# Halved last residuals, row sums taken from the loaded input, a two-engine tail and half copies in attention D of a three-layer block

## The chip, the cores and the metric

The kernel runs on one core of a Trainium2 chip. The metric is the device time of one execution in microseconds. All data are float32. TensorE makes the matrix products into PSUM, ScalarE (ACT) and VectorE (DVE) read PSUM and work on it, GpSimd (POOL) splits weights and activations, and SyncE (SP) issues most DMAs.

## The reference

Three layers on a residual stream `h` of 1024 tokens by 1024 features. The first is a four-branch mixer with a feed-forward part, then come one even and one odd attention layer, ahead of which the first block's result is normalized again:

```
h = x
xn = rmsnorm(h, norm_mix_w);  proj = xn @ w_in       # four gated branches
h = h + merged @ w_out
xn = rmsnorm(h, norm_ffn_w);  g, u = split(xn @ w_ffn_in)
h = h + (silu(g) * u) @ w_ffn_out
x = rmsnorm(h, norm_f_w)
x = x + (cat(attention A, attention B) * silu(gate)) @ w_out_e     # even layer
x = x + (cat(attention C, attention D) * silu(gate)) @ w_out_o     # odd layer
```

where `rmsnorm(x, w) = x * rsqrt(mean(x * x) + 1e-6) * w` over the features. Attention D is a differential attention with four heads:

```
p = softmax(q1 @ k1.T * scale) - lam * softmax(q2 @ k2.T * scale);  o = rmsnorm(p @ v)
```

Its queries and keys are projections of the normalized stream, normalized per head and partly rotated.

## The kernel before

The stream lies transposed in SBUF as `H`, eight tiles of 128 features by 1024 tokens. `A(i)` is one of 29 work buffers of that shape. PSUM is used as four banks of 128 x 1024, given out in turn to numbered jobs (`opn`). The last writer of a bank raises `filled`, its last reader raises `freed`, and job n waits for job n - 4 to be freed. Every engine has its program written out in order, and the engines meet only in semaphores.

A product in full precision is made of three: weights and activations are split into a high part (`WH`, `XH`) and a low part (`WL`, `XL`), and 8 x 3 x 2 = 48 matmuls of 512 columns make a tile (`three`, `split_gemm`, `xgemm`, `xhalves`; 24 or 36 where fewer feature tiles go in). SP loads each weight into one of four slots of `WR`; POOL casts it to `WH` (line 3145) and subtracts to `WL` (3147), which lies over `WR`, so a slot is free again when its product is done. `xhalves` gives the same product in two steps of 24 matmuls, one for each half of the tokens. `XL` lies over `H`: before it is written, all of `H` is stored to `spill` in HBM, and it is loaded back later.

At the start the eight tiles of `x` are loaded and transposed by TensorE (470). ScalarE copies each to `H` (1467) and squares four (1474), VectorE squares the other four (2260), and TensorE sums the squares with 64 matmuls (481). A matmul of plain float32 data stands as two passes in the trace; a transpose, and a matmul of split data, as one.

A norm (numbers 0, 1, 3 and 4 in the code) goes as follows. VectorE adds each residual tile (`residual_norm`), ScalarE squares it and stores it (`square`, 1425; in norm 3 there is a second square without weights, 1433, for the final norm of the first block), VectorE sums the squares over the tiles into `A(28)` (and `A(16)`), and TensorE sums over the partitions (`sums`, 431). ScalarE seeds the root (1417, 1419), VectorE refines it in three steps (`newton`), and TensorE spreads it over the partitions (`spread`, 449). VectorE scales (2268), ScalarE casts to `XH` (1440, 1443, 1447), and VectorE and POOL subtract to `XL` by turns. The first pair of products behind a norm, `two_after_norm` (331, 338, 345), takes up each tile as it comes.

The attentions are woven by hand: each step of the attention's loop is followed on every engine by one step of the preparation of the next head (`weave`). In D a head has 16 such steps. TensorE's `prep_d_halves` (404) makes the first half of the keys in step 0 and the second in step 2, and the queries in steps 4 and 6; then come the sums (`hn`). ScalarE's `prep_d_halves` copies and squares the whole tile in steps 3 and 7 by `raw` (1809, 1811), and only then is the bank freed:

```
act.activation(dst[0:m, :], t[0:m, :], ACT.Copy, scale=gain)
act.activation(sq[0:m, :], t[0:m, :], ACT.Square).then_inc(freed[bank(name)], 1)
```

At the end TensorE transposes `H` back, eight transposes for each of eight token tiles (1300), and ScalarE copies each tile out of PSUM (2244) and issues its store (2247).

## Time and profile before

| | |
|---|---|
| median of 3 runs | 3924.49 us (3920.34 to 3936.52) |
| profiled execution | 3924.81 us, span 3923.0 us |
| granted TensorE clock, mean | 0.984 of full |
| TensorE matmul busy | 3751.3 us, 96% |
| VectorE busy | 1818.7 us, 46% |
| ScalarE busy | 1295.7 us, 33% |
| GpSimd busy | 916.9 us, 23% |
| DMA | 215.32 MB, mean 55 GB/s |

The profile is one execution. The span is the time between the first and the last instruction in it. Busy shares are averages over stages with different limits, so what an edit is worth is read at its own place.

### The profile page before, as it was taken

How to read it: one execution, taken by the hardware profiler on the slowest of the kernel's cores; microseconds unless marked ns; L12 is line 12 of the kernel's file. 1: busy time of each engine (PE TensorE's matmuls, PEld its weight loads, DVE VectorE, ACT ScalarE, POOL GpSimd, SP SyncE). 2: the span in 40 equal slices, each digit the busy share in tenths (PEclk: the TensorE clock that was granted, in tenths of full speed). 3: DMA queues.
4: the chain of work that ended last, by engine and by line, in shares of the span. 5: the costliest groups of instructions: out<-in, count | busy, mean ns of one | idle time of the engine just before them, and what ended most of it. 6: DMA issues, size and time to landing. Idle time of an engine off the chain costs nothing.

```text
span 3923.0 us, 51837 instructions
## 1 busy us (share of the span) xinstructions
PE 3751.3 (96%) x21792; PEld 2959.3 (75%) x21792; DVE 1818.7 (46%) x2309; ACT 1295.7 (33%) x1523; POOL 916.9 (23%) x558
## 2 busy tenths in 40 slices
PE   8999999999999999999999999999999999999988
PEld 7778888877788878888888767677676566667767
DVE  6464455624643622101102555655744555456672
ACT  3243333332330111001001234455623666444441
POOL 4212222222233424333333411110023001111101
PEclk9999999999999999999999999999999999999999
DMA  4111111111125421111113221100112001111011
GB/s 144 33 44 54 44 54 44 49 54 46 44 91 185 137 86 43 48 49 48 49 49 103 79 57 48 38 22 7 52 58 62 14 13 26 30 25 25 17 54 68
DMA packets 276813, 215.32 MB, mean 55 GB/s; under 512 B 16273, under 2 KB 255025, under 8 KB 276593
## 3 DMA queue, kind: packets, MB, share of 16 engines
q1 hardware_dynamic: 257808, 150.31, 13.4%
q10 hardware_dynamic: 18784, 61.88, 4.5%
q8 instruction: 163, 2.67, 0.3%
q14 instruction: 58, 0.47, 0.0%
HBM read 170.27 MB, written 37.81 MB: 53 GB/s over the span
## 4 chain that ended last, share of the span: by engine, by line
PE 83%; DVE 9%; ACT 4%; issue 3%; ACTq 0%; DMA 0%; DVEq 0%; SPq 0%
PE ps L356 30%; PE ps L373 17%; PE ps L404 15%; DVE AR L2260 3%; PE ps L1166 2%; DVE SM L3019 2%; PE ps L635 2%; DVE AR L2268 1%; PE ps L338 1%; PE ps L1177 1%; PE ps L1157 1%; PE ps L309 1%; PE ps L449 1%; PE ps L1188 1%; PE ps L1237 1%
## 5 line engine op out<-in xcount | busy, mean ns | idle before, releaser
L3145 POOL CAST WH<-WR 128x1024 fp32r<-128x1024 f32 (+2 forms) x269 | 283.3, 1053 | 2869.2 <-DMA WR<-in_w_in 828.7
L3147 POOL TENSOR_TENSOR WL<-WR,WH 128x1024 fp32r<-128x1024 f32 (+2 forms) x269 | 595.0, 2212 | 21.5
L356 PE MATMUL ps<-XH,WH 128*128 128x512 f32 x1776 | 450.2, 396 | 2.3 <-DVE AR L2260 1.7
L356 PE MATMUL ps<-XH,WL 128*128 128x512 f32 x1776 | 440.5, 390 | 0.0
L356 PE MATMUL ps<-XL,WH 128*128 128x512 f32 x1776 | 438.8, 389 | 0.0
L2260 DVE TENSOR_TENSOR AR<-AR 128x512 f32<-128x512 f32 (+3 forms) x336 | 378.0, 1125 | 54.1 <-ACT AR L1668 38.1
L373 PE MATMUL ps<-ARR,WH 128*128 128x512 f32 x1600 | 395.5, 389 | 5.6 <-ACT ARR L1774 3.4
L356 PEld LDWEIGHTS ps<-XH,WH 128*128 128x128 f32 x1776 | 330.6, 188 | 78.9 <-issue 5.0
L356 PEld LDWEIGHTS ps<-XH,WL 128*128 128x128 f32 x1776 | 332.6, 187 | 72.7
L356 PEld LDWEIGHTS ps<-XL,WH 128*128 128x128 f32 x1776 | 331.1, 186 | 71.8
L373 PEld LDWEIGHTS ps<-ARR,WH 128*128 128x128 f32 x1600 | 300.4, 188 | 69.6 <-ACT ARR L1774 4.6
L2260 DVE TENSOR_TENSOR AR<-AR,ps 128x1024 f32<-128x1024 f32 (+2 forms) x72 | 84.7, 1176 | 550.7 <-PE ps L356 409.3
L3019 DVE TENSOR_REDUCE SM<-ps 128x1 f32<-128x1024 f32 x128 | 156.7, 1224 | 197.9 <-PE ps L1166 116.8
L404 PE MATMUL ps<-XH,WH 128*128 128x512 f32 x864 | 234.6, 415 | 2.9 <-ACT AR L2099 2.3
L2268 DVE SCALAR_TENSOR_TENSOR AR<-ps,AR 128x512 f32<-128x512 f32 (+2 forms) x122 | 59.3, 486 | 343.2 <-ACT AR L1419 228.9
L404 PE MATMUL ps<-XH,WL 128*128 128x512 f32 x864 | 214.1, 390 | 0.0
L404 PE MATMUL ps<-XL,WH 128*128 128x512 f32 x864 | 213.4, 389 | 0.0
L1783 ACT ACTIVATE AR<-ps 128x1024 f32<-128x1024 f32 x22 | 22.6, 1027 | 558.4 <-PE ps L356 558.4
L404 PEld LDWEIGHTS ps<-XH,WH 128*128 128x128 f32 x864 | 159.8, 195 | 56.2 <-issue 19.7
L404 PEld LDWEIGHTS ps<-XH,WL 128*128 128x128 f32 x864 | 162.7, 188 | 34.8
L373 PE MATMUL ps<-ARR,WL 128*128 128x512 f32 x736 | 187.7, 389 | 0.0
L404 PEld LDWEIGHTS ps<-XL,WH 128*128 128x128 f32 x864 | 162.2, 188 | 33.7
(261 smaller groups left out, 5165.6 us busy)
## 6 DMA issues: line engine op xcount, KB each, us to landing
WR<-in_w_in SPq DMA_DIRECT2D x78, 512.0 KB, 3.8
WR<-in_w_ffn_in SPq DMA_DIRECT2D x44, 512.0 KB, 3.8
gates<-AR ACTq DMA_DIRECT2D x32, 512.0 KB, 2.9
AR<-gates SPq DMA_DIRECT2D x32, 512.0 KB, 3.6
H<-spill ACTq DMA_DIRECT2D x32, 512.0 KB, 5.5
WR<-in_w_in_e SPq DMA_DIRECT2D x26, 512.0 KB, 3.9
spill<-H ACTq DMA_DIRECT2D x24, 512.0 KB, 2.6
WR<-in_w_in_o SPq DMA_DIRECT2D x23, 512.0 KB, 3.8
```

What stands on the lines that cost most here:

```text
L309: mm = pe.matmul(pt[0:m, h * 512:h * 512 + 512], WR[0:kp, w % 4, k, 0:m], rhs(k)[0:kp, h * 512:h * 512 + 512], start=k == 0, stop=k == nk - 1)
L338: pe.matmul(pt[:, h * 512:h * 512 + 512], wp[:, slot, k, :], XH[:, k, h * 512:h * 512 + 512], start=False, stop=False, skip_group_check=True)
L356: mm = pe.matmul(pt[0:m, h * 512:h * 512 + 512], wp[:, slot, k, 0:m], xp[:, k, h * 512:h * 512 + 512], start=i == 0, stop=i == 3 * KD - 1)
L373: mm = pe.matmul(pt[:, h * 512:h * 512 + 512], wp[:, w % 4, k, :], xp(k)[:, h * 512:h * 512 + 512], start=i == 0, stop=i == 3 * nk - 1)
L404: mm = pe.matmul(pt[:, h * 512:h * 512 + 512], wp[:, w % 4, k, :], xp[:, k, h * 512:h * 512 + 512], start=i == 0, stop=i == 3 * KD - 1)
L635: mm = pe.matmul(out, x1[r, c], later, start=True, stop=True)
L1166: mm = pe.matmul(pt[:, h * 512:h * 512 + 512], q(p, m)[0:96, rows], k(p, m)[0:96, h * 512:h * 512 + 512], start=True, stop=True)
L2260: return v.tensor_tensor(o, x, y, op)
L2268: return v.scalar_tensor_tensor(out=o, in0=x, scalar=s, in1=y, op0=op0, op1=op1)
L3019: v.tensor_reduce(SM[:, 34 + m:35 + m], PS[bank(("S", b, m))][:, :], AX.X, ALU.max)\
L3145: pool.tensor_copy(hi, full).then_inc(s_whi, 1)
L3147: pool.tensor_tensor(lo, full, hi, ALU.subtract).then_inc(s_wsplit, 1)
```

## The change

At the start ScalarE squares the loaded tiles as they lie, token by partition, with a row sum into one column each, and a single transpose of these columns takes the place of the 64 matmuls. VectorE makes all eight copies to `H`. The mask is loaded behind two weights, and `two_after_norm` waits for each weight's split by itself. In the norms 1, 3 and 4 the last residual tile is added in two halves, the first when the first half of its product is done; TensorE sums the first seven tiles' squares and the last one's as separate groups. In norm 3 the sums for the final norm move behind the first pair of products. At the end seven eighths of the first three tiles are transposed ahead of the last residual, ScalarE and VectorE copy by turns, and SP issues the stores. In attention D, ScalarE takes the halves of keys and queries each behind its own half product.

```diff
-                pe.wait_ge(s_wsplit, nsplit[0])
                 splits.append(("norm", norm))
                 for h in range(2):
                     pe.wait_ge(s_xhi if h else s_xhi_half, t * KD + 1 if h else t + 1)
-                    for pt, n, slot in places:
+                    for j, (pt, n, slot) in enumerate(places):
+                        if not h:
+                            pe.wait_ge(s_wsplit, nsplit[0] - 1 + j)
...
+                    if halves and h == 0:
+                        mm.then_inc(s_half_done, 1)
...
+                    if not h and first_done is not None:
+                        mm.then_inc(first_done, 1)
...
-                pe.wait_ge(s_sumsq, norm_turn(i) * (KD - 1))
+                t = norm_turn(i)
+                pt, n = opn(("norm", i))
+                pe.wait_ge(freed[n % 4], n // 4)
+
+                def add(kind, x, first, last):
+                    c = CW[kind]
+                    for j in range(4):
+                        for g in range(2):
+                            mm = pe.matmul(pt[g * 64:g * 64 + 64, 0:P], CST[:, c + 6 - 2 * j:c + 70 - 2 * j],
+                                           x[:, (4 * g + j) * P:(4 * g + j + 1) * P], start=first and j == 0, stop=last and j == 3)
+                    return mm
+
+                pe.wait_ge(s_sumsq, t * (KD - 2))
+                add("w1024", A(28), True, False)
                 if i == 3:
-                    pe.wait_ge(s_sumsq_plain, KD - 1)
-                    sums(("norm", 3), ("w1024", "weps"), [A(28), A(16)])
-                    sums(("norm_f",), "w1024", [A(16)])
-                else:
-                    sums(("norm", i), "w1024", [A(28)])
+                    pe.wait_ge(s_sumsq_plain, KD - 2)
+                    add("weps", A(16), False, False)
+                pe.wait_ge(s_nsq, t * (KD + 1))
+                mm = add("w1024", A(27), False, i != 3)
+                if i == 3:
+                    pe.wait_ge(s_nsq_plain, KD + 1)
+                    mm = add("weps", A(18), False, True)
+                mm.then_inc(filled[n % 4], 1)
...
-            for t in range(NT):
-                g, i, c = t // 4, t % 4, CW["w1024"]
-                if t in DVE_SQUARES:
-                    pe.wait_ge(s_xsq, DVE_SQUARES.index(t) + 1)
-                else:
-                    pe.wait_ge(freed[bank(("x", t))], turn(("x", t)))
-                for f in range(KD):
-                    mm = pe.matmul(pt[g * 64:g * 64 + 64, 0:P], CST[:, c + 6 - 2 * i:c + 70 - 2 * i],
-                                   A(16 + t)[:, f * P:f * P + P], start=i == 0 and f == 0, stop=i == 3 and f == KD - 1,
-                                   skip_group_check=True)
-            mm.then_inc(filled[n % 4], 1)
+            pe.wait_ge(s_xsq, NT)
+            pe.transpose(pt[:, 0:P], A(26)[:, 0:P], IDENT).then_inc(filled[n % 4], 1)
...
+                sums(("norm_f",), "w1024", [A(16), A(18)])
+                xgemm(("va", 0), cols(wie, EVA))
                 spread(("norm_fb",), A(19))
-                xgemm(("va", 0), cols(wie, EVA))
...
-            for k in range(4):
-                n = J["wout_o"] + 4 + k
+            for k in range(3, 7):
+                n = J["wout_o"] + k
                 pe.wait_ge(freed[n % 4], n // 4 + 1)
-            for t in range(NT):
+
+            def turn_out(t, fs):
+                pt, n = PS[bank(("out", t))], J[("out", t)]
+                for f in fs:
+                    mm = pe.transpose(pt[:, f * P:f * P + P], H[:, f, t * P:t * P + P], IDENT)
+                return mm, n
+
+            for t in range(3):
+                opn(("out", t))
+                turn_out(t, range(KD - 1))
+            pe.wait_ge(s_half_added, 4)
+            for t in range(3):
+                mm, n = turn_out(t, [KD - 1])
+                mm.then_inc(filled[n % 4], 1)
+            n = J["wout_o"] + 7
+            pe.wait_ge(freed[n % 4], n // 4 + 1)
+            for t in range(3, NT):
                 pt, n = opn(("out", t))
                 pe.wait_ge(freed[n % 4], n // 4)
-                for f in range(KD):
-                    mm = pe.transpose(pt[:, f * P:f * P + P], H[:, f, t * P:t * P + P], IDENT)
+                mm, n = turn_out(t, range(KD))
...
+                if w == 2 and not mask_in:
+                    sp.dma_start(MSK[:, :, :].rearrange("p a b -> p (a b)"), a["msk"]).then_inc(s_msk_in, 16)
+                    mask_in.append(True)
...
+            for t in range(NT):
+                sp.wait_ge(freed[bank(("out", t))], turn(("out", t)))
+                sp.dma_start(a["out"][0, t * P:t * P + P, :], A(16 + t)).then_inc(s_out_in, 16)
+            sp.wait_ge(s_out_in, 16 * NT)
...
-            def square(i, k):
-                if k >= 3:
-                    act.wait_ge(s_sumsq, (norm_turn(i) - 1) * (KD - 1) + k - 2)
-                act.activation(A(26 + k % 2) if k else A(28), H[:, k, :], ACT.Square,
+            def square(i, k, c=slice(0, L), last=True):
+                t = norm_turn(i) - 1
+                if k >= 3 and c.start == 0:
+                    act.wait_ge(s_sumsq, t * (KD - 2) + k - 2)
+                act.activation((A(26 + k % 2) if k else A(28))[:, c], H[:, k, c], ACT.Square,
                                scale=par("nf", k) if i == 3 else 1.0).then_inc(s_nsq, 1)
                 act.wait_ge(s_nsq, tick(s_nsq))
                 if i == 3:
                     if k == 0:
                         act.wait_ge(s_part, KD)
-                    if k >= 3:
+                    if k >= 3 and c.start == 0:
                         act.wait_ge(s_sumsq_plain, k - 2)
-                    act.activation(A(17 + k % 2) if k else A(16), H[:, k, :], ACT.Square).then_inc(s_nsq_plain, 1)
+                    act.activation((A(17 + k % 2) if k else A(16))[:, c], H[:, k, c], ACT.Square).then_inc(s_nsq_plain, 1)
                     act.wait_ge(s_nsq_plain, tick(s_nsq_plain))
-                act.dma_start(a["spill"][k], H[:, k, :]).then_inc(s_spilled, 16)
+                if last:
+                    act.dma_start(a["spill"][k], H[:, k, :]).then_inc(s_spilled, 16)
...
+                    if k == KD - 1:
+                        act.wait_ge(s_half_added, norm_turn(i))
+                        square(i, k, slice(0, 512), False)
                     act.wait_ge(freed[n % 4], n // 4 + 1)
-                    square(i, k)
+                    square(i, k, slice(512 if k == KD - 1 else 0, L))
...
+            logs()
+            act.wait_ge(s_xsq_zero, 1)
             for t in range(NT):
-                act.wait_ge(filled[bank(("x", t))], turn(("x", t)))
-                pt = PS[bank(("x", t))]
-                copy = act.activation(H[:, :, t * P:t * P + P], pt[:, :].rearrange("p (f i) -> p f i", i=P), ACT.Copy)
-                if t in DVE_SQUARES:
-                    copy.then_inc(freed[bank(("x", t))], 1)
-                    act.wait_ge(freed[bank(("x", t))], turn(("x", t)))
-                else:
-                    copy.then_inc(s_act_step, 1)
-                    act.wait_ge(s_act_step, tick(s_act_step))
-                    act.activation(A(16 + t), pt[:, :], ACT.Square).then_inc(freed[bank(("x", t))], 1)
-                    act.wait_ge(freed[bank(("x", t))], turn(("x", t)))
-            logs()
-            act.wait_ge(s_par_in, 32)
+                act.wait_ge(x_in[t], 16)
+                c = 64 * (t // 4) + 2 * (t % 4)
+                act.activation(A(16 + t), A(t), ACT.Square, scale=1.0 / 32, accum_out=A(26)[:, c:c + 1]).then_inc(s_xsq, 1)
+                act.wait_ge(s_xsq, tick(s_xsq))
...
+            def first_half(name, nth, dst, sq=None, gain=1.0):
+                act.wait_ge(s_d_half, nth)
+                t = PS[bank(name)]
+                act.activation(dst[:, 0:512], t[:, 0:512], ACT.Copy, scale=gain).then_inc(s_act_step, 1)
+                act.wait_ge(s_act_step, tick(s_act_step))
+                if sq is not None:
+                    act.activation(sq[:, 0:512], t[:, 0:512], ACT.Square).then_inc(s_act_step, 1)
+                    act.wait_ge(s_act_step, tick(s_act_step))
+
+            def second_half(name, dst, sq=None, gain=1.0):
+                act.wait_ge(filled[bank(name)], turn(name))
+                t = PS[bank(name)]
+                last = act.activation(dst[:, 512:L], t[:, 512:L], ACT.Copy, scale=gain)
+                if sq is not None:
+                    last.then_inc(s_act_step, 1)
+                    act.wait_ge(s_act_step, tick(s_act_step))
+                    last = act.activation(sq[:, 512:L], t[:, 512:L], ACT.Square)
+                last.then_inc(freed[bank(name)], 1)
+                act.wait_ge(freed[bank(name)], turn(name))
+
             def prep_d_halves(h):
-                yield from pause(3)
+                k, q = A(10 + h % 2), A(8 + h % 2)
+                yield
                 act.wait_ge(s_rope_tmp, 14 + 2 * h)
-                raw(("kd", h), A(10 + h % 2), A(22), gain=par("gkd"))
-                yield
-                rotated(A(28), A(10 + h % 2), (0, 64), 8, s_rot_in[1])
-                yield from pause(3)
-                raw(("qd", h), A(8 + h % 2), A(7), gain=par("gqd"))
+                first_half(("kd", h), 2 * h - 1, k, A(22), par("gkd"))
+                yield from pause(2)
+                second_half(("kd", h), k, A(22), par("gkd"))
+                yield
+                rotated(A(28), k, (0, 64), 8, s_rot_in[1])
+                yield
+                first_half(("qd", h), 2 * h, q, A(7), par("gqd"))
+                yield from pause(2)
+                second_half(("qd", h), q, A(7), par("gqd"))
                 root()
                 yield
-                rotated(A(27), A(8 + h % 2), (0, 64), 8, s_rot_in[0])
+                rotated(A(27), q, (0, 64), 8, s_rot_in[0])
...
+            def last_residual(n, nth, between):
+                v.wait_ge(s_half_done, nth)
+                TT(H[:, KD - 1, 0:512], H[:, KD - 1, 0:512], PS[n % 4][:, 0:512], ALU.add).then_inc(s_half_added, 1)
+                v.wait_ge(s_half_added, nth)
+                between()
+                v.wait_ge(filled[n % 4], n // 4 + 1)
+                TT(H[:, KD - 1, 512:L], H[:, KD - 1, 512:L], PS[n % 4][:, 512:L], ALU.add).then_inc(freed[n % 4], 1)
+                v.wait_ge(freed[n % 4], n // 4 + 1)
...
+                    if k == KD - 1:
+                        last_residual(n, norm_turn(i), lambda: add_square(i, KD - 2))
+                        continue
...
+            v.memset(A(26)[:, 0:P], 0.0).then_inc(s_xsq_zero, 1)
+            v.wait_ge(s_xsq_zero, 1)
+            for t in range(NT):
+                v.wait_ge(filled[bank(("x", t))], turn(("x", t)))
+                v.tensor_copy(H[:, :, t * P:t * P + P], PS[bank(("x", t))][:, :].rearrange("p (f i) -> p f i", i=P))\
+                    .then_inc(freed[bank(("x", t))], 1)
...
+            for t in range(1, NT, 2):
+                v.wait_ge(filled[bank(("out", t))], turn(("out", t)))
+                v.tensor_copy(A(16 + t), PS[bank(("out", t))][:, :]).then_inc(freed[bank(("out", t))], 1)
+                v.wait_ge(freed[bank(("out", t))], turn(("out", t)))
```

Of the pieces with `if k == KD - 1`, the first is in ScalarE's `norm_after`, the second in VectorE's `residual_norm`. The last product ahead of each norm is called with `halves` set. ScalarE's `prep_a0` now takes queries and keys first, then the seeds of the final norm, and then the bias load (`in_rpb`), which came first before.

How the rows of TensorE's program stand around norm 3 (`L373`/`L378` is the last product ahead of it, `L431`/`L440`/`L470` are summing matmuls and `L449`/`L458` spreads), before:

```order
L373 MATMUL ps<-ARR_54,WH 128x512 x2
L431 MATMUL ps<-AR,CST 64x128 x24
L449 MATMUL ps<-AR,CST 128x128 x8
...
L345 MATMUL ps<-XL,WH 128x512 x32
L449 MATMUL ps<-AR,CST 128x128 x8
L356 MATMUL ps<-XH,WH 128x512 x8
```

and in the changed kernel:

```order
L378 MATMUL ps<-ARR_54,WH 128x512 x2
L470 MATMUL ps<-AR,CST 64x128 x32
L458 MATMUL ps<-AR,CST 128x128 x8
...
L350 MATMUL ps<-XL,WH 128x512 x32
L440 MATMUL ps<-AR,CST 64x128 x16
L361 MATMUL ps<-XH,WH 128x512 x8
```

There are 32 summing matmuls ahead of the spread where 24 stood, and 16 behind the pair of products where the second spread stood.

ScalarE's program at the start of attention D (`L2139`/`L2200` are the exponentials, `L2128`/`L2189` copies of turned probabilities, and the rows with `PAR` copies of keys), before:

```order
L2139 ACTIVATE AR,SM<-ps,SM,AR 128x1024 x4
L1809 ACTIVATE AR<-ps,PAR 128x1024
L1811 ACTIVATE AR<-ps 128x1024
L2128 ACTIVATE AR<-ps 128x1024
L1803 DMA AR<-AR 8x1024
```

and in the changed kernel:

```order
L2200 ACTIVATE AR,SM<-ps,SM,AR 128x1024 x2
L2112 ACTIVATE AR<-ps,PAR 128x512
L2115 ACTIVATE AR<-ps 128x512
L2200 ACTIVATE AR,SM<-ps,SM,AR 128x1024 x2
L2121 ACTIVATE AR<-ps,PAR 128x512
L2125 ACTIVATE AR<-ps 128x512
L2189 ACTIVATE AR<-ps 128x1024
L1835 DMA AR<-AR 8x1024
```

The first half of the keys stands between the first two pairs of exponentials, the second half where the whole pair stood.

## Rows read from the trace of the kernel before

**Rows 1.** The page, busy time by engine: us, share, instructions

```profile
PE 3751.3 (96%) x21792; PEld 2959.3 (75%) x21792; DVE 1818.7 (46%) x2309; ACT 1295.7 (33%) x1523; POOL 916.9 (23%) x558
```

**Rows 2.** Chain that ended last, 0 to 70 us: start, us, what

```profile
18.07 13.82 PE ps L481 x128
...
36.70 3.75 PE ps L331 x8
...
61.58 8.61 PE ps L356 x38
```

**Rows 3.** Timeline of the start: start, us, instructions, [idle before <-releaser]

```profile
14.99 2.12 PE L470 MATMUL ps<-CST,AR 128*128 128x128 f32 x16 [0.46 <-ACT AR L1474]
...
19.05 1.04 POOL L3145 CAST WH<-WR 128x1024 fp32r<-128x1024 f32 x1 [18.60 <-DMA WR<-in_w_in]
...
20.17 3.21 POOL L3147 TENSOR_TENSOR WL<-WR,WH 128x1024 fp32r<-128x1024 f32 x1
...
50.28 3.24 POOL L3147 TENSOR_TENSOR WL<-WR,WH 128x1024 fp32r<-128x1024 f32 x1
```

**Rows 4.** Windows at the start: length, busy by engine, then clock, DMA share, GB/s

```profile
31.00:32.00 1.00, 0.88 (x9) 0.63 (x6) 0.00 (x0) 0.03 (x1) 0.00 (x0) 1.00 1.04 414
...
33.00:34.00 1.00, 0.21 (x2) 0.21 (x4) 0.67 (x3) 0.00 (x0) 0.00 (x0) 1.00 0.57 221
```

**Rows 5.** Groups of instructions by shape: busy, mean ns | idle before

```profile
L2703 DVE COPY AR<-ps 128x1024 f32<-128x1024 f32 x8 | 9.8, 1224 | 76.0 <-PE ps L373 76.0
...
L1440 ACT ACTIVATE XH<-AR 128x512 fp32r<-128x512 f32 x4 | 2.5, 630 | 14.8 <-DVE AR L2268 14.8
```

**Rows 6.** Chain of norm 1: start, us, what

```profile
1455.48 1.23 DVE H L2260
...
1459.27 1.97 PE ps L431 x16
...
1463.08 2.10 PE ps L449 x16
```

**Rows 7.** One window of norm 1, columns as in rows 4

```profile
1459.00:1460.00 1.00, 0.73 (x8) 0.73 (x10) 0.21 (x1) 0.46 (x1) 0.00 (x0) 0.67 0.90 369
```

**Rows 8.** Chain of norm 3 and behind it: start, us, what

```profile
2198.87 3.70 PE ps L431 x32
...
2204.40 1.19 PE ps L449 x16
...
2242.93 1.02 PE ps L431 x16
```

**Rows 9.** TensorE's waits, whole span: us in total, times, longest

```profile
PE ps L431 <- DVE AR L2260: 7.9, 2, 3.9
...
PE ps L431 <- issue: 6.5, 1, 6.5
```

**Rows 10.** TensorE's waits in attention D, columns as in rows 9

```profile
PE ps L431 <- ACT AR L1811: 7.8, 3, 2.7
...
PE ps L1237 <- ACT AR L1811: 1.5, 1, 1.5
...
PE ps L1223 <- ACT AR L1811: 1.3, 2, 0.6
```

**Rows 11.** Timeline of attention D, first head: ScalarE and VectorE

```profile
3491.26 1.02 ACT L2128 ACTIVATE AR<-ps 128x1024 f32<-128x1024 f32 x1 [3.13 <-PE ps L1223]
...
3500.78 1.11 ACT L1809 ACTIVATE AR<-ps,PAR 128x1024 f32<-128x1024 f32 x1
...
3502.34 1.28 DVE L2268 SCALAR_TENSOR_TENSOR AR<-AR,SM 128x1024 f32<-128x1024 f32 x1
```

**Rows 12.** Timeline of the tail

```profile
3907.66 6.30 PE L1300 MATMUL ps<-CST,H 128*128 128x128 f32 x56 [1.61 <-DVE H L2260]
...
3908.82 1.02 ACT L2244 ACTIVATE AR<-ps 128x1024 f32<-128x1024 f32 x1 [53.60 <-PE ps L1300]
3909.87 0.34 ACTq L2247 DMA_DIRECT2D out<-AR  x1
```

**Rows 13.** DMA queue, 3900 to 3923 us: packets, MB, share of 16 engines

```profile
q10 hardware_dynamic: 1152, 4.19, 45.6%
```

49 lines of the change are left out of this document (25 added, 24 removed).

## The prediction

> **What bounds the kernel now.** I read the busy shares first. TensorE is busy for 96% of the span [rows 1] and no other engine for half of it, so a change pays only where TensorE stands waiting, and there it pays in full, because what follows is packed TensorE work. I then listed TensorE's waits. The places that the diff touches are on that list, and I read the chain of each.
>
> At the start TensorE spends 13.82 us on 128 passes of square sums, the first product starts at 36.70, and the first pair of products ends at 61.58 [rows 2]. At norm 1 the last product ends at 1455.35, 0.13 ahead of the residual add; three VectorE passes follow, the sums run from 1459.27 to 1461.24, and the spread takes 2.10 [rows 6]. The same wait of 3.9 stands twice in the list, for norm 1 and norm 4 [rows 9]. At norm 3 the wait is 6.5, and 32 passes of sums take 3.70 [rows 8, 9]. In D TensorE waits 7.8 us in three places and 2.8 in three more for ScalarE's square of keys or queries, line 1811 [rows 10]. In the tail eight copies and stores stand one behind the other on ScalarE.
>
> **The start.** Removed: 64 summing matmuls (13.82) and ScalarE's copies. Added: eight squares with a row sum on ScalarE straight from the loaded tiles, eight PSUM copies on VectorE, one transpose. A VectorE copy of this shape takes 1.22 [rows 5]. The last two tiles are turned from 14.99 on, in 2.12 us, with hardly a gap [rows 3], so the last tile lands at about 16.0. The last copy then ends at 18.4, and the last square at 17.3. What the row sum costs is not shown for this form: from nothing to the square's own time again for one tile, 18.3. From there the old steps remain: root, spread, first scale and cast took 36.70 − 31.89 = 4.8. TensorE could start at about 22.5.
>
> It then needs split weights. The first came in at 19.05 and took 1.04 + 3.21 to split [rows 3]. With the 512 KB mask behind two weights, both land 1.3 us earlier at 414 GB/s [rows 4]. Weight 1 is split at about 21.3 to 22.1, weight 2 at 25 to 26.5. The new wait is per weight, so two products (0.9 us) fit between, and TensorE ends the pair 24.9 (61.58 − 36.70) after 24 to 25.6, at 49 to 50.5.
>
> What is late next is the low parts. They are written over H, so they wait for the store of H, and the DMA engines are full until 33.6 [rows 4]. The change moves the same bytes, so that end stays. VectorE and GpSimd then start four low parts each, side by side, where GpSimd's subtract takes 3.24 [rows 3]. So GpSimd is done at 33.6 + 4 × 3.3 = 46.8, just in time for TensorE. Only then does it split weight 3, 1.04 + 2.4, until 50.5. The third product starts at 50.6 against 61.58: **11.0 saved**. Bounds: 9 if every GpSimd step has its slow price, 13 if the store ends earlier.
>
> **Norms 1 and 4.** The last residual is added in two halves, the first half and its square beside the second half of the product. That half lasts at least 2.7 us (norm 4: 12 matmuls of 8.61/38 = 0.227 [rows 2]); the first half's add (0.7) and the waiting sum pass (1.24) fit in it. Behind the product remain 0.13, a half add of about 0.68 (half of 1.23 and a fixed part), a half square (the cast of that shape takes 0.63 [rows 5]) and about 0.08 of hand-over, 1.5 in all, then 16 passes. Where TensorE had just worked these took 1.02 [rows 8]; the other 16 run before. They end 2.5 behind the product, against 1461.24 − 1455.35 = 5.9: 3.4 saved. The spread took 2.10 at norm 1 and 1.19 at norm 3 [rows 6, 8], half and full clock. TensorE's first idle stretch shrinks from 3.9 to 0.5, so I take full clock: 0.9. **4.3 each, 8.6 for both.** The clock fell to half within the 1459 to 1460 row, four us after the last product [rows 7].
>
> **Norm 3.** Four groups of 16 passes now stand on the path, 4.1 us at full clock, three of them able to run while VectorE and ScalarE finish their halves (0.13 + 0.68 + 2 × 0.63 + 0.08 = 2.2). The sums end 4.1 behind the product, against 6.5 + 3.7 = 10.2: 6.1 saved. The sums of the final norm come later, two groups behind the first pair of products: 2.0 of TensorE added. **Net 4.1.** The bias load and its two VectorE adds move behind keys and queries, four full copies of about 1.03 on ScalarE, so 4 us later. The gate's product, 48 matmuls or 10.9 us, covers them, so I cost them at nothing; without that cover they would cost up to 4.
>
> **Attention D.** For each of three heads ScalarE now copies and squares the first halves while TensorE makes the second half product, and only two half-size instructions stay behind it. A full pair took 1.11 + 1.03 [rows 11]. A half from PSUM is not shown. Its bounds are half of that and all of it; I take 0.63 each, the cast's row [rows 5]: 1.3 against 2.2, 0.9 saved behind every product. For keys the waits of 1.5, 0.65 and 0.65 shrink by 0.9, 0.65, 0.65. For queries 2.6 shrinks by 0.9 in two heads; in the first the probabilities come only at 3503.62 [rows 11], 0.5 behind today's start of the sums, so 0.5. That is 4.5, and I take **4.0** for new small delays. The new first halves stand where ScalarE idles: 3.13 us ahead of the next copy at the place of the first head's queries [rows 11]. Bounds: 0, if ScalarE's next copy is delayed as often as a wait is cut, and 5.
>
> **The tail.** Three tiles are transposed for seven eighths ahead of the last residual. But 21 transposes of 6.30/56 = 0.11 take 2.4 us, so the first copy starts 2.6 behind the last product, against 2.76 now (3908.82 − 3906.06) [rows 12]. What shrinks is the stretch after it: copies on two engines and stores from SyncE come every 0.7 us and not every 1.44, and then the DMA engines bind. Today 13.1 us pass from the first store to the end; the transfers fill 45.6% of 23 us, 10.5 us, of it [rows 13]. Packed, with 0.8 for the first and last edge, they take 11.3. **Saved 1.9**, bounds 0 and 3.
>
> The Trainium skill speaks against that term: "DMA: Bandwidth & Descriptors", section "Where 436 GB/s comes from", says that transfers between HBM and SBUF are held to some 358 GB/s. By it the 4.19 MB take 11.7 us, the tail gives 0.7, and the result would be 3896. The row of 414 GB/s in a store to HBM contradicts it [rows 4], so the row decides.
>
> **Sum.** 11.0 + 8.6 + 4.1 + 4.0 + 1.9 = 29.6. The profiled execution took 3924.8 us (span 3923.0 and 1.8 around it), 0.3 above the median of the runs. 3924.8 − 29.6 = 3895.2, so **3895 us**.
>
> **Rivals.**
> - *The clock.* It was down when the sums began at norms 1 and 3 [rows 7, 8]. If it still is, the sums cost 1.0 more and the spreads 0.9 more in norms 1 and 4, and norm 3 up to 3.9 more: 3895 + 7.7 = 3903. If it never falls, the first eight products take 1.8 in place of 3.75 [rows 2] and the next five 1.1 less: 3 us twice and some 1.5 at norm 3, so 3887. For the first speaks that only small matmuls with gaps fill the stretch; against it, that the idle is shorter. The Trainium skill, "TensorE: Matmul & The Clock Gate", Part 1, calls the throttled clock the default that activity releases; that leaves both open.
> - *The start gives less.* If the store of H ends later (its issue now stands behind a VectorE copy) or the low parts slow each other further, the third product comes at 55 and D gives nothing: 3895 + 4.4 + 4.0 = 3903.
> - *Attention D turns slower and eats everything.* ScalarE works in order. At six places it now waits for a half product, with the next copy of turned probabilities and the exponentials queued behind it, for which TensorE waits. If each wait held the attention back by a whole half product, 24 × 0.23 = 5.5 us, that is 33, against 25.6 saved elsewhere: 3895 + 4 + 33 = 3932, slower than before. It decides from 4.3 us per place. Against it: the half product is issued a half step earlier, and the idle stretch of 3.13.
> - *The wait moves in norm 3.* The bias adds come too late: 4 us, 3899, inside the forecast's own range.
>
> **How the numbers follow.** Forecast 0.62 (3889 to 3901), clock down or a poorer start 0.20 (3901 to 3908), clock never down or the store earlier 0.12 (3882 to 3889), D slower 0.03, the rest 0.03. The range 3885 to 3906 leaves out some 2 in 10. Half a per cent, 20 us, is about what a measurement of this kernel tells from no change; the gain falls under it only in the last two cases and in a pile of misses. Faster 0.93, same 0.04, slower 0.03.
>
> **What the profile after would show.** The third product near 50.6, behind GpSimd's split and not behind the input. In norms 1 and 4 the sums end 2.5 behind the last product and the spread takes 1.2; the granted clock tells which case it is. In norm 3 no row at half clock in the sums. In D no wait for the square of keys in the second and third head, and 1.7 in place of 2.6 for queries. In the tail a solid stretch of DMA at over 400 GB/s. The prediction is wrong if TensorE waits at a new place: for first halves in D, for the bias in norm 3, or for the third weight beyond 52.

## The result and the profile after

The changed kernel takes 3909.41 us (median of 5 runs, 3899.55 to 3914.30), beside 3923.89 for the kernel before in the same rounds: a ratio of 0.9949 with a 95% interval of 0.9932 to 0.9966. It is faster by 14.5 us at the medians, half of the 29.6 that the prediction summed up, and the time lies 3.4 us above the upper end of its range, 3906. The profiled execution took 3912.17 us with a span of 3910.3, so the two spans that are compared here differ by 12.7.

It was timed again in two later batches, 6 runs each: 0.9956 (0.9942 to 0.9971) and 0.9937 (0.9920 to 0.9954). A least-squares fit over all runs of all kernels, with one level for each batch, gives the change a gain of **20.8 us, plus or minus 3.0** (17 runs of it, 61 of the kernel before). One run scatters by 5.2 us (standard deviation) whatever the kernel. So the forecast of 29.6 is some 9 us too high. That the first five runs were poor ones isn't shown: 14.5 and 20.8 differ by no more than five runs on either side allow.

First the page of the changed kernel, busy time by engine, to lay beside [rows 1]:

```profile
PE 3745.8 (96%) x21745; PEld 2950.7 (75%) x21745; DVE 1848.5 (47%) x2318; ACT 1291.3 (33%) x1538; POOL 908.8 (23%) x558
```

TensorE is busy for 5.5 us less, and the rest of the 12.7 is waiting that went away. VectorE works 30 us more.

**The start**, the chain that ended last (start, us, what), beside [rows 2]:

```profile
11.78 1.23 DVE H L2414
...
18.07 1.24 DVE H L2414
...
25.11 10.36 DMA spill<-H
...
35.59 2.39 POOL XL L3235
...
44.74 3.26 POOL XL L3235
...
48.06 1.92 POOL WH L3225
...
50.05 2.38 POOL WL L3227
...
52.56 17.51 PE ps L361 x76
```

The 13.82 us of square sums are gone; VectorE's eight copies end at 19.3. The chain then leaves TensorE: the last store of H lands at 35.46, four low parts follow, then the split of weight 3, and only then the third product, at 52.56 instead of 61.58. The prediction had this chain, with a landing at 33.6 and a cast of 1.04.

TensorE itself is close behind. Its timeline around the start of the first pair of products and around its end, with GpSimd and VectorE between 18 and 23 us:

```profile
22.48 2.08 PE L458 MATMUL ps<-AR,CST 64*128 64x128 f32 x16 [5.18 <-DVE AR L2327]
26.42 0.76 PE L336 MATMUL ps<-XH,WH 128*128 128x512 f32 x1 [1.86 <-ACT XH L1481]
...
43.78 7.42 PE L350 MATMUL ps<-XL,WH 128*128 128x512 f32 x32
...
52.56 2.08 PE L361 MATMUL ps<-XH,WH 128*128 128x512 f32 x8 [1.37 <-POOL WL L3227]
```

```profile
18.84 2.34 POOL L3227 TENSOR_TENSOR WL<-WR,WH 128x1024 fp32r<-128x1024 f32 x1
...
19.65 2.77 DVE L2327 SCALAR_TENSOR_TENSOR AR<-AR 128x128 f32<-128x128 f32 x2
```

The pair begins at 26.42, not between 24 and 25.6, and ends at 51.20. So GpSimd's chain holds the third product back by 1.4 us and no more.

**Norm 1**, the chain from the last product on, beside [rows 6]:

```profile
1456.61 0.70 DVE H L2319
...
1457.39 0.64 ACT AR L1465
...
1458.40 1.28 ACT L1445
...
1459.70 0.38 ACT AR L1456
...
1461.52 1.30 PE ps L458 x16
...
1464.65 3.75 PE ps L336 x8
```

One full add, one full square and one full sum have become halves. In their place ScalarE's table load (L1445, 1.28) now stands on the chain; before, it began at 1458.17, beside VectorE's pass, and the sums ended 1.8 us behind it.

**Norm 3**, TensorE's timeline, beside [rows 8]:

```profile
2189.33 3.71 PE L470 MATMUL ps<-AR,CST 128*64 128x128 f32 x64
2194.91 1.16 PE L458 MATMUL ps<-AR,CST 64*128 64x128 f32 x16 [1.87 <-DVE AR L2327]
```

The sums begin right behind the last product and not 6.5 us later, and 64 passes take 3.71, as long as 32 took before at half clock [rows 8].

**The merge ahead of norm 1** is a place that the change doesn't touch. TensorE's waits there, 1340 to 1378 us, in the kernel before and in the changed one (us, times, longest):

```profile
PE ps L373 <- ACT ARR L1765: 2.2, 1, 2.2
```

```profile
PE ps L378 <- ACT ARR L1803: 4.9, 2, 4.8
```

**Where the 12.7 are.** I took the same TensorE instruction in both traces and subtracted the start times. The change is ahead by 8.9 us at 62, 8.6 at 285, 3.8 at 1350, and it is *behind* by 1.0 at 1373. From there it gains 3.5 around norm 1, 3.5 around norm 3, 3.0 in the stretch with norm 4, 3.2 in attention D. So in this pair of traces each of these places gains, and 9.5 us vanish between 285 and 1373, in code that is the same in both.

**Theories.** A: the gain of the start is real, but is given back between 285 and 1373, because everything there runs in another phase (other waits, another order of VectorE and GpSimd, other falls of the clock). B: nothing is given back; single executions differ by this much in that stretch, and the profile of before was a good one. C: the local gains are an illusion of alignment, and the start is all there is.

### The profile page after: what moved, and what is told of

The parts are those of the page before. It is cut to its first block, busy times and chain, and to the rows that moved or that the text cites. A ratio compares the mean times of both kernels' runs of the same rounds, so it can differ in the third digit from the quotient of the medians.

```text
span 3910.3 us, 51791 instructions
## 1 busy us (share of the span) xinstructions
PE 3745.8 (96%) x21745; PEld 2950.7 (75%) x21745; DVE 1848.5 (47%) x2318; ACT 1291.3 (33%) x1538; POOL 908.8 (23%) x558
## 4 chain that ended last, share of the span: by engine, by line
PE 83%; DVE 9%; ACT 4%; issue 3%; POOL 0%; DMA 0%; ACTq 0%; SPq 0%; DVEq 0%; POOLq 0%
PE ps L361 30%; PE ps L378 17%; PE ps L411 15%; DVE AR L2319 2%; PE ps L1183 2%; DVE SM L3092 2%; PE ps L651 2%; DVE AR L2327 1%; PE ps L1194 1%; PE ps L1174 1%; PE ps L1205 1%; PE ps L313 1%; PE ps L458 1%; PE ps L1254 1%; PE ps L343 1%
## 5 line engine op out<-in xcount | busy, mean ns | idle before, releaser
L378 PE MATMUL ps<-ARR,WH 128*128 128x512 f32 x1600 | 396.0, 390 | 8.3 <-ACT ARR L1803 4.9
L378 PEld LDWEIGHTS ps<-ARR,WH 128*128 128x128 f32 x1600 | 300.4, 188 | 72.6 <-ACT ARR L1803 5.7
L378 PE MATMUL ps<-ARR,WL 128*128 128x512 f32 x736 | 189.3, 392 | 0.0
```

Source lines behind the costliest of these rows:

```text
L378: mm = pe.matmul(pt[:, h * 512:h * 512 + 512], wp[:, w % 4, k, :], xp(k)[:, h * 512:h * 512 + 512], start=i == 0, stop=i == 3 * nk - 1)
```

## The experiments

**The change in three parts.** Each kernel is that of before with the diff's blocks of one part: `start_only` (norm 0, copies, mask, waits by weight), `norms_only` (norms 1, 3, 4), `d_tail` (attention D and the tail). Their core:

```
start_only   + act.activation(A(16 + t), A(t), ACT.Square, scale=1.0 / 32, accum_out=...)
             - for t in DVE_SQUARES: ...
norms_only   + last_residual(n, norm_turn(i), lambda: add_square(i, KD - 2))
d_tail       + first_half(("kd", h), ...); second_half(...)
             + for t in range(1, NT, 2): v.tensor_copy(A(16 + t), ...)
```

> Only the start of the change: norm 0 from squares of x itself, first-tile waits one by one, mask load behind the second weight. Nothing else differs from the kernel before. Theory A (the start's gain is real, but is given back in unchanged code between 285 and 1373 us, by other waits on VectorE and clock falls at other places): the third product starts 8 to 10 us earlier, at 1373 us no more than 2 us of it is left, and the time is within 3 us of the kernel before. Theory B (the gain stays, and what the whole change lacked is chance of the clock in single executions): at 1373 us and at the end 7 to 10 us are left, time 3914 to 3917 when the kernel before has 3924. Theory C (the norms and D gave nothing and the start is all that was gained): 12 to 15 us faster.

> Only norms 1, 3 and 4 are changed (halved last residual and square, one addition fewer, sums in two parts, final norm's sums behind the first product); the start, attention D and the tail are as before. Theory A: nothing is saved up to 1455 us, then about 3 us at norm 1, 6.4 at norm 3 and 4 at norm 4, together 13 to 14 us, all of it still there at the end (3910 when the kernel before has 3924). Theory B: the same 13 to 14 us. Theory C: under 3 us. If a gain ahead of a stage is given back there in general (theory A carried further), less than 9 us stay at the end though the three places show their 13.

> Only attention D (first halves of keys and queries copied and squared behind their own half product) and the tail (halved last residual, output tiles copied by ScalarE and VectorE in turn, stores by SyncE) are changed. Theories A and B: nothing up to 3372 us, then 3.5 us in attention D and 1.2 to 1.9 us in the tail, 4.5 to 5.5 us in all (3919 when the kernel before has 3924). Theory C: under 1 us. Rival to both: D's gain in the whole change came from another phase of the weave, and alone the change of D gives 0 or a loss of 1 to 3 us.

> The changed kernel once more, in the same rounds as its three parts, for its time beside theirs and for a second profiled execution. If the parts add up, its gain is the sum of the gains of the three partial kernels to within 3 us. Theory A: 14 to 18 us faster than before, and the loss between 285 and 1373 us stands in this execution too, by 6 to 10 us. Theory B: a profiled execution with less time at half clock keeps 7 us or more of the start at 1373 us.

Measured against 29 runs of the kernel before (3926.25):

```
kernel        median    ratio (95%)
start_only    3921.46   0.9986 (0.9973 to 0.9998)
norms_only    3919.75   0.9987 (0.9975 to 0.9998)
d_tail        3923.30   0.9992 (0.9981 to 1.0004)
after_again   3909.53   0.9956 (0.9942 to 0.9971)
```

The fit over all batches gives 5.6, 7.2 and 3.6 us, each plus or minus 3.6: together 16.4 against 20.8, the same within the scatter. The norms alone gain more than theory C allows (under 3 us in its own condition), and the start alone gains far less than its 12 to 15, so C falls. The gain of `d_tail` is not clear of zero in its time. Two expectations missed: `norms_only` was to give 13 to 14 us and gave 7.2, and `start_only` fell between the ranges of theories A and B. `start_only` is ahead by 9.1 us at 62 and 3.2 at 1373, which looks like theory A. But `d_tail`, which equals the kernel before up to 3372 us, is 8.7 us behind it at 1350, and `norms_only` 3.4. That is what theory B says. In the one trace of `norms_only` 11.1 us stand in the three stretches with a norm, and 8.4 of them are left at the end, because of the stretch ahead of 1373.

**Who comes first, VectorE or GpSimd.** In the merge, VectorE adds the last branch to the accumulator while GpSimd splits the first weights of the output product. VectorE's and GpSimd's timelines of the changed kernel, 1350 to 1360 us (start, us, instruction):

```profile
1351.91 2.00 DVE L2319 TENSOR_TENSOR ACC<-ACC,AR 128x1024 f32<-128x1024 f32 x1
1353.94 3.31 DVE L2319 TENSOR_TENSOR XH<-ACC,ARR 128x1024 fp32r<-128x1024 f32 x1
...
1358.54 3.17 DVE L2319 TENSOR_TENSOR ACC<-ACC,AR 128x1024 f32<-128x1024 f32 x1
```

```profile
1351.79 1.04 POOL L3225 CAST WH<-WR 128x1024 fp32r<-128x1024 f32 x1 [6.43 <-DMA WR<-in_w_out]
1352.91 3.26 POOL L3227 TENSOR_TENSOR WL<-WR,WH 128x1024 fp32r<-128x1024 f32 x1
```

The same two engines in the first profile of the kernel before:

```profile
1355.73 1.22 DVE L2260 TENSOR_TENSOR ACC<-ACC,AR 128x1024 f32<-128x1024 f32 x1
1356.99 1.95 DVE L2260 TENSOR_TENSOR XH<-ACC,ARR 128x1024 fp32r<-128x1024 f32 x1
...
1361.17 1.23 DVE L2260 TENSOR_TENSOR ACC<-ACC,AR 128x1024 f32<-128x1024 f32 x1
```

```profile
1355.81 2.04 POOL L3145 CAST WH<-WR 128x1024 fp32r<-128x1024 f32 x1 [6.63 <-DMA WR<-in_w_out]
```

Read the starts. Where GpSimd's cast begins 0.12 us ahead of VectorE's add, it takes 1.04 and the add 2.00; the next two adds of SBUF tiles are the second ones too, and need up to 3.31 for 1.22 us of work. Where it begins 0.08 us behind, the cast takes 2.04 and the add its 1.22. The blocked instruction ends 1.08 us after the other in both of the first pairs (1351.79 + 1.04, then 1353.91; 1352.91 + 3.26, then 1357.25), so it waits for the whole of it. The Trainium skill, "SBUF — State Buffer", section "Who interferes with whom", states that a VectorE instruction with two SBUF inputs contends with a GpSimd instruction that reads SBUF, and that issue order decides who blocks. By that rule, the trace agrees: an add that reads PSUM and one SBUF tile keeps its 1.22 at 1357.29, beside GpSimd's cast of 1.92 at 1356.24.

Three edits follow. `merge_order` makes GpSimd wait with that split for VectorE's sixth add, and moves the table load of norm 1 up:

```
+ if w == first_wout[0]:
+     pool.wait_ge(s_acc, 2 * KD + 6)
...
+ logs()
  norm_after("wout", 1)
```

`late_split` puts a wait into the kernel before, which lets GpSimd begin with the seventh product, so that its subtraction comes just ahead of VectorE's add:

```
+ if w == first_wout[0]:
+     n = J[("br", 3, 6)]
+     pool.wait_ge(filled[n % 4], n // 4 + 1)
```

`spill_both` tests the start. It is the changed kernel, with the odd stores of H issued by ScalarE instead of SyncE:

```
- for k in range(KD):
+ for k in range(0, KD, 2):
      sp.dma_start(a["spill"][k], H[:, k, :]).then_inc(s_spilled, 16)
...
+ for k in range(1, KD, 2):
+     act.dma_start(a["spill"][k], H[:, k, :]).then_inc(s_spilled, 16)
```

`all_three` is the changed kernel with this edit and both edits of `merge_order`.

> The changed kernel, but the eight stores of the residual at the start are issued by two engines: SyncE the even tiles, ScalarE the odd ones, between its seed for norm 0 and its wait for the first normalised half, where it stood idle for 7.4 us. Theory A (the start gave 8.9 and not 11.0 us because SyncE took 6.45 us to issue the eight stores, so that the last landed at 35.46 and not at 33.6 us, and GpSimd's low parts, the split of weight 3 and the third product wait for it in a chain): the stores land 1.5 to 3 us earlier, GpSimd's first low part starts so much earlier, the third product starts at 50 to 51 us instead of 52.56. Rival (the transfer itself is bound by its rate, 4 MB whoever issues it): the last store lands within 0.5 us of 35.46 and the third product stays at 52 to 53 us. The time as a whole: up to 2 us faster than the changed kernel, which five rounds can hardly tell.

> The changed kernel with two edits at two places: GpSimd splits the first weight of the output product only when VectorE has added the sixth tile of the last branch (one wait), and ScalarE loads its table for logarithm and exponential ahead of the squares of norm 1 instead of between the last square and the seed. Theory A (in the changed kernel GpSimd's first split began 0.12 us ahead of VectorE's addition, and from there on VectorE's additions had to wait for GpSimd's: 2.0 to 3.2 us instead of 1.22; before it began 0.08 us behind it, and GpSimd's were the ones that waited): the additions on that chain fall back to 1.2 to 2.0 us, TensorE's wait for the last merged tile falls from 4.8 to 2.2 us, 3 to 4 us are kept at 1372 us. Rival (the additions are slow for what they touch, or TensorE's product ends late for another reason): the wait stays at 4 to 5 us. For the table: if it is exposed, 1.28 us disappear between the last square and the logarithm and norm 1 ends 0.6 to 1.3 us earlier; if the sums on TensorE end no earlier than the table, nothing. The time: 3 to 5 us faster than the changed kernel, 3904 to 3907 when that has 3909.

> The changed kernel with all three: stores on two engines, the ordered split and the earlier table. Theory A: the three gains add, 2 + 3.5 + 1 us, 3901 to 3905 when the changed kernel has 3909 and the kernel before 3926, a ratio of 0.993 to 0.995. Rival (a gain ahead of 1373 us is not kept, since the order of VectorE and GpSimd and the clock fall differently in each program): within 3 us of the changed kernel.

> The kernel before with one wait more: GpSimd begins the split of the first weight of the output product only when the seventh product of the last branch is done, 4 us later than it does by itself, so that its subtraction begins just ahead of VectorE's addition of that tile instead of behind it. No product waits for this split (it is needed some 10 us later). Theory A (who begins first decides): VectorE's additions beside the splits grow from 1.22 to 2 us and more, TensorE's wait for the last merged tile grows from 2.2 to 4 or 5 us, 2 to 3 us are lost at 1372 us. Rival (the order does not matter, or the split is only needed later): the wait stays at 2.2 us. Up to 1350 us the kernel is that of before, so its profile is also a second look at the stretch from 285 to 1350 us: if the profile of before was a lucky one there, this one is 4 us or more behind it at 1000 us.

Measured against 15 runs of the kernel before (3928.17):

```
kernel        median    ratio (95%)                 lost 1350-1373   TensorE's wait
spill_both    3906.04   0.9940 (0.9927 to 0.9954)   4.8              4.8
merge_order   3903.11   0.9938 (0.9924 to 0.9951)   1.5              2.4
all_three     3904.70   0.9947 (0.9933 to 0.9960)   0.9              2.4
late_split    3925.94   1.0000 (0.9991 to 1.0009)   3.5              4.2
```

The order decides the wait, shown from both sides: put right, the wait is 2.4 in `merge_order` and `all_three`, put wrong, it is 4.2. VectorE's rows of `late_split`:

```profile
1360.26 3.33 DVE L2262 TENSOR_TENSOR ACC<-ACC,AR 128x1024 f32<-128x1024 f32 x1
1363.62 1.95 DVE L2262 TENSOR_TENSOR XH<-ACC,ARR 128x1024 fp32r<-128x1024 f32 x1
```

and of `merge_order`:

```profile
1358.24 1.51 DVE L2322 TENSOR_TENSOR ACC<-ACC,AR 128x1024 f32<-128x1024 f32 x1
1359.79 1.95 DVE L2322 TENSOR_TENSOR XH<-ACC,ARR 128x1024 fp32r<-128x1024 f32 x1
```

In `late_split` the add grew from 1.22 to 3.33 and TensorE's wait to 4.2, as theory A's price for the order had it, though nothing waits for the split itself. That place cost it 3.5 us in the trace, but its time of 1.0000 doesn't show them. Its interval reaches to 3.5 us, just so, and the kernel before, against which it is timed, falls into the same order in some of its own executions (below).

The start, GpSimd's rows of `spill_both`:

```profile
34.82 12.41 POOL L3240 TENSOR_TENSOR XL<-AR,XH 128x1024 fp32r<-128x1024 f32 x4 [10.32 <-DMA spill<-H]
47.30 1.91 POOL L3230 CAST WH<-WR 128x1024 fp32r<-128x1024 f32 x1
49.29 2.37 POOL L3232 TENSOR_TENSOR WL<-WR,WH 128x1024 fp32r<-128x1024 f32 x1
```

The low parts begin 0.8 us earlier (34.82 instead of 35.59) and the third product at 51.81. But `merge_order`, where SyncE alone issues the stores and needs 7.22 us for it, begins them at 34.88. So two issuing engines bring nothing, and theory A of that expectation (1.5 to 3 us earlier) fell. The rival's numbers were a little off too: the last store lands at 34.70, 0.76 ahead of 35.46, and the third product comes at 51.81 and not at 52 to 53. But its cause holds, that the issue does not set the landing, and the kernel before shows it best. There the last store is issued at 29.0, 3.9 us later than in the changed kernel, and this is its row and the time to its landing:

```profile
L1344 SPq DMA_DIRECT2D spill<-H x1: 1204/1204/1204, 29.0 to 29.0; - x1
...
DMA to landing us min/median/max: 6.3/6.3/6.3
```

It lands at 35.3, where those of the changed kernel land. The low parts begin between 34.8 and 35.6 in every kernel with the new start.

The table: behind the last square the logarithm begins 1.68 us after in the changed kernel and 1.18 after in the second execution of the ordered one (below), so 0.5 us of the 1.28 were exposed. `all_three` is no faster than either of its parts: 22.8 us ahead of the kernel before in the fit, beside 23.0 for `spill_both`, each plus or minus 5.2.

**Chance or program.** So far the changed kernel, `spill_both` counted with it, had come out badly at the merge in three executions of three, and the kernel before, with its three parts, well in four of four. So both ran again, unchanged (`before_again`, `after_third`), the ordered kernel as `order_again`, and `start_norms`, which is the changed kernel without the blocks of attention D and the tail:

```
- first_half(("kd", h), ...); second_half(...)
+ raw(("kd", h), A(10 + h % 2), A(22), gain=par("gkd"))
- for t in range(1, NT, 2): v.tensor_copy(A(16 + t), ...)
```

> The kernel before, unchanged, for one more profiled execution of it. If the profile of before was ahead of its usual course between 285 and 1350 us (which the kernels that equal it there were behind by 1.2 to 10 us), this one is behind it by 2 to 8 us at 1350 us, and GpSimd's first split of the output weights begins just behind VectorE's addition (wait of TensorE 2.2 us). If it is within 1 us of the first profile all along, the stretch costs the other kernels something that their code brings.

> The changed kernel without its edits in attention D and in the tail, that is the start and the norms together. If the start and the norms are what puts GpSimd's split ahead of VectorE's addition, TensorE's wait for the last merged tile is 4.8 us as in the changed kernel, and the time is 4 us above it (3 of attention D and 1.3 of the tail). If it takes the whole program, the wait is 2.2 us, 3.5 us of the race come back and the time is within 1 us of the changed kernel: 3909 to 3910 when that has 3909.

> The changed kernel once more, as the base for the ordered one on the same chip. 16 to 19 us faster than the kernel before; GpSimd's split ahead of VectorE's addition and TensorE's wait of 4.8 us once more, if this belongs to the program and not to chance in one execution.

> The changed kernel with the ordered split and the earlier table, once more and beside the changed kernel on the same chip. 3.5 us from the order and 0.6 us from the table: 4 us faster than the changed kernel (2 to 6 with the spread of five rounds), 20 to 23 us faster than the kernel before. If the clock takes the gain back elsewhere, it is within 1 us of the changed kernel.

Measured against 11 runs of the kernel before (3929.89); the first is a single execution:

```
kernel        median    ratio (95%)                 lost 1350-1373   TensorE's wait
before_again  3931.39   -                           4.8              4.8
start_norms   3910.14   0.9954 (0.9939 to 0.9968)   4.7              4.8
after_third   3902.68   0.9937 (0.9920 to 0.9954)   1.2              2.2
order_again   3906.78   0.9939 (0.9926 to 0.9952)   0.2              2.4
```

The same program of the kernel before now has, at the same place:

```profile
1353.96 1.04 POOL L3145 CAST WH<-WR 128x1024 fp32r<-128x1024 f32 x1 [6.41 <-DMA WR<-in_w_out]
1354.10 1.98 DVE L2260 TENSOR_TENSOR ACC<-ACC,AR 128x1024 f32<-128x1024 f32 x1
```

and the changed kernel, in its third execution:

```profile
1351.59 1.23 DVE L2319 TENSOR_TENSOR ACC<-ACC,AR 128x1024 f32<-128x1024 f32 x1
1351.70 2.02 POOL L3225 CAST WH<-WR 128x1024 fp32r<-128x1024 f32 x1 [6.66 <-DMA WR<-in_w_out]
```

So one and the same program does both. It is a toss in each execution, and it goes with the time that the weight takes from its issue to its landing: 4.7 to 4.8 us in the five executions that came out badly, 4.9 to 5.3 in the five that came out well, among the ten without a wait of mine there. Theory A's mechanism is right, and its claim that the change brings the bad order about each time is wrong. Whether the change shifts the odds stays open: four of six executions with the new start came out badly and one of four without it, too few to tell. My expectation for `before_again` named only the better case, and missed; so did the one for `after_third`, which had the wait of 4.8 and 16 to 19 us. Against the first profile of before, the second one is 3.1 us behind at 1373 and 6.6 at the end.

The ordered kernel (`merge_order`, `order_again`) is 23.1 us faster than the kernel before in the fit, plus or minus 3.8, the changed one 20.8 plus or minus 3.0. It never lost the toss in three executions, `all_three` among them, but 2 us can't be told from none here. The expectation for `order_again`, 4 us faster than the changed kernel, missed: on that chip the changed kernel's median was 4.1 us lower. That the order is worth its 3.5 us in the time is not shown.

**All traces together.** With fourteen traces each stretch can be taken as a mean over the kernels that have an edit, less the mean over those that don't. All are differences to the first trace of before, in us, with twice the standard error:

```
stretch (us of before)      with edit    without     edit's gain      forecast
0-62       the start         9.30 (9)     0.47 (5)    8.8 +- 0.5       11.0
62-285                      -0.59        -0.14       -0.4 +- 0.5        0
285-1350                    -2.78        -2.22       -0.6 +- 4.2        0
1373-1473  norm 1            3.72 (9)     0.76 (5)    3.0 +- 0.7        4.3
2190-2245  norm 3            3.51         0.58        2.9 +- 0.3        4.1
2900-3372  norm 4            4.56        -0.34        4.9 +- 1.6        4.3
3372-3852  attention D       3.41 (8)    -0.69 (6)    4.1 +- 1.5        4.0
3852-end   the tail         -0.31        -0.97        0.7 +- 1.1        1.9
```

The third row bears on theory A: kernels with the new start lose 2.8 us between 285 and 1350 beside the first profile of before, kernels without it 2.2. A give-back is not shown there, and up to some 5 us of it can't be excluded. Single executions of code that is the same reach from 8.7 behind to 1.6 ahead in that stretch, which is enough to make the 4.8 us that the first pair of traces lost there. The local gains sum to 23.4 (with -1.0 for the second and third rows, and without stretches that no edit touches), which the timing's 20.8 plus or minus 3.0 holds.

## Where the prediction was right and where it was wrong, by its steps

The direction and the places were right. The sum of 29.6 was too large by some 9 us, above all in the terms of the start and of the norms 1 and 3.

- **The start, 11.0 forecast, 8.8 measured.** The chain was right: the third product comes behind GpSimd's split, not behind the input. "The change moves the same bytes, so that end stays" was right too: the last store lands at 35.3 before and at 34.7 to 35.5 with the change. What failed is the time that was read for it. 33.6 is where the DMA share falls off [rows 4], and the landing, which is what GpSimd waits for, comes 1.7 us behind that. The step of 46.8 to 50.5 also had a cast of 1.04 where 1.92 was measured: it begins beside VectorE's last low part (45.77 to 49.07), as the uncontended row I took [rows 3] did not. The low parts gave 0.8 back, 12.41 for four instead of 13.2. A second step failed beside it, and would have held the third product at 51.2 even with a landing at 33.6: the pair of products was to begin at 24 to 25.6 and began at 26.42. "Root, spread, first scale and cast took 4.8" was read where GpSimd stood still. Now VectorE's last two steps of the root run beside GpSimd's split and take 2.77 instead of 0.62, and the spread behind them takes 2.08 instead of 1.19, at a granted clock of 0.50 between 20 and 26 us. They end at 21.33 and 22.42, 0.15 and 0.14 behind the GpSimd instructions beside them (21.18 and 22.28), and in all nine traces with the new start the two take 2.6 to 3.5: by these ends it is the same blocking as in the merge, on the path of the start. No run took it away.
- **Norm 1, 4.3 forecast, 3.0 measured; norm 4, 4.3 forecast.** From the last product's last matmul to the next product's first, norm 1 went from 11.1 to 12.1 us in the five executions without the edit to 8.45 to 8.96 with it, norm 4 from 12.0 or 12.1 to between 7.9 and 8.5, a gain of 3.9 in the mean. So the forecast holds within 0.4 at norm 4. (The two kernels that load the table early are left out at norm 1; three executions of them took 8.1 to 8.9.) At norm 1 a cover was overlooked: the table load lay beside VectorE's pass that the change takes off the path, and 0.5 us of it came out. The rest goes in part to the spread, which took 1.30 in the changed kernel's first execution and up to 2.10, at half clock, in `order_again`, where 1.2 was forecast: the clock rival at one place.
- **Norm 3, 4.1 forecast, 2.9 measured.** The 6.1 in the wait and sums is right: 15.3 us became 8.9, that is 6.4. The moved sums of the final norm cost the 2.0 that were forecast (32 passes, 1.97). What was missed is 1.0 us of clock: the first two products took 24.4 instead of 23.4, because the granted clock, which before was 0.50 for 6 us under the sums and again for the first 3 us of the products, is now 1.00 under the sums and 0.50 for the first 5 us of the products (2198 to 2203). The clock can be moved off a cheap stretch onto a dear one. The bias adds cost nothing, as forecast: TensorE's waits behind them are 4.5 and 1.5 us, and were 4.7 and 1.5 before.
- **Attention D, 4.0 forecast, 4.1 plus or minus 1.5.** TensorE's waits for ScalarE there were 7.8, 1.5 and 1.3 [rows 10], and in the changed kernel:

```profile
PE ps L440 <- ACT AR L2125: 5.1, 3, 1.7
...
PE ps L1254 <- ACT AR L2125: 0.6, 1, 0.6
```

  That is 4.9 less, the longest wait for queries at the forecast 1.7. Keys have no wait left but one of 0.6. The rival in which D turns slower fell: no wait for a first half is on the list.
- **The tail, 1.9 forecast, 0.7 plus or minus 1.1.** From the last product's end to the end of the span it is 16.9 before (3906.06 to 3923.0) and 15.9 after (3894.4 to 3910.3). Windows of the changed kernel's tail (columns as in [rows 4]):

```profile
3900.00:3902.00 2.00, 1.86 (x18) 1.62 (x15) 1.26 (x2) 1.28 (x2) 0.00 (x0) 1.00 1.01 404
3902.00:3904.00 2.00, 0.00 (x0) 0.00 (x0) 1.19 (x1) 0.11 (x1) 0.00 (x0) 1.00 1.03 408
3904.00:3906.00 2.00, 0.00 (x0) 0.00 (x0) 0.00 (x0) 0.00 (x0) 0.00 (x0) 1.00 1.02 404
```

  The transfers are packed, as forecast, and at over 400 GB/s, so the trace decides against the 358 GB/s that the Trainium skill states ("DMA: Bandwidth & Descriptors", "Where 436 GB/s comes from"). What was too small are the edges: 12.2 us pass from the first store to the end, of which 10.5 are transfer, so 1.7 and not 0.8. Over all traces the tail's gain is not clear of zero.
- **The base.** 2 us more come from the profiled execution that the sum was made against. It took 3924.8, the mean level of before in the fit is 3926.7 to 3928.5.

Together the local terms were 5 to 6 us too high, and the base 2 too low. That is 3902 to 3903 for 3895; the changed kernel's 17 runs have a mean of 3906.7. The last 4 us are not accounted for; they lie within the errors of the stretches, of which one alone has 4.2. The prediction's range also left out that a single execution scatters by 5 us.

## What to carry to other kernels

Compare stretches only with a second profile of the kernel *before*: without one, 9.5 us that single executions scatter by anyway looked like a loss in code that nobody had touched. Read a wait for a store from the landing of the store, not from the place where the DMA share falls off: here 1.7 us lay between them. When an instruction is taken off the path, list what lay beside it (here a table load and a stretch at half clock), because that is on the path next, and ask what runs beside the new path that did not run beside the old one (here GpSimd's splits, beside the root and the low parts). Where VectorE and GpSimd run chains of two-input operations side by side, look at the first pair's start times: 0.1 us decided 2.6 us of TensorE's waiting (4.8 instead of 2.2), and one wait set the order in three executions of three.

## What the runs showed of the hardware

- A VectorE add of two SBUF tiles and a GpSimd cast or subtract wait for each other over whole instructions (the blocked one ended 1.08 us behind the other twice), and the order carries over to the next pairs: one toss at 1351 us made three of VectorE's adds take 2.0 to 3.3 us instead of 1.22. An add with one input in PSUM kept its 1.22. What makes the weight land 0.2 us earlier in one execution than in the next stays open.
- A single execution of one program scatters by 5.2 us (0.13%, a standard deviation), and this goes with the mean granted clock: over the runs of all kernels in the first two batches, 0.001 of clock goes with 3.4 us.
- Eight stores of 512 KB to HBM issued by one engine in 7.2 us or by two in 2.5 landed at the same time, 0.1 us apart, and so did those of the kernel before, whose last one was issued at 29.0 and not at 25.8 (35.3 beside 34.7 to 35.5).
- A row sum with a ScalarE square of 128x1024 costs an instruction of its own of 0.18 us behind the square's 1.06; the prediction had allowed up to the square's time once more.
